# Attention stage of a hybrid decoder step: order of turns, scores and minima in each quarter, and a new split of the PSUM banks

## The chip, the cores and the metric

The kernel runs on one core of one Trainium2 chip. The metric is the device time of one launch in microseconds (us), lower is better. Engines are called PE (TensorE; PEld is its weight load), DVE (VectorE), ACT (ScalarE), POOL (GpSimd) and SP (SyncE).

## The reference, cut to what matters

One layer of a Hymba-style decoder over a prompt of 1024 tokens and a sample batch of 8 x 4 tokens. The change touches only the prompt's attention:

```
qs = q * (HEAD_DIM ** -0.5)
# per head and block of 128 queries:
o_cmp = softmax(qs k_cmp + bias, masked) v_cmp          # 16 compressed blocks
o_sel = softmax(qs k_sel + bias, masked) v_sel          # selected blocks; 16 blocks, so all are selected
o_win = softmax(qs k_win + bias, masked) v_win          # 512 back plus the own block
out   = g0 * o_cmp + g1 * o_sel + g2 * o_win            # g = sigmoid gates; 16 heads of 64
mix   = out * silu(z_a)
```

All is in fp32; the score products use a high and a low part of the keys.

## The kernel before, in words

Before the stage come the projections (up to 890 us of the span) and the compressed blocks; after it the sample's attention and the output projection (from 1443 us). The prompt's attention lies between.

**Units.** The stage has NU = 32 units. Unit u works on 4 heads (pass u // 8 of four) and the 128 queries of block i = TILE_ORDER[u % 8], in the order 0, 2, 4, 6, 7, 5, 3, 1. Each unit has two halves, numbered w: w = 2u is the selected branch with i + 1 tiles of 128 keys, w = 2u + 1 is the window branch with min(i + 1, 5) tiles and one tile for the compressed blocks (`tiles_of`, `keys_of`). So a pass has 74 tiles. Each half is cut into four quarters h = 0 to 3, one for each head's scores, and the half's tiles are dealt out over the quarters (`slots`).

**What is done for a half w.** `scores(w, h)`, on PE, multiplies one head's queries with up to 1024 keys into a score buffer. `maxima(w, h)`, on DVE, adds the bias to the last 256 columns and takes the minimum (scores are negated); `exps(w, h)`, on ACT, takes the exponential into the SBUF tile pr and the sum. When all four heads are done, `factors(w)`, on DVE, makes gate over sum, and `scale` multiplies pr by it: heads 0 and 1 on POOL, 2 and 3 on ACT. Then `turn_p(w, t)`, on PE, transposes the four heads' 128 columns of tile t into a PSUM bank ("turned"), `copy_p(w, t)` copies this bank to the SBUF tile ptt (even tiles on ACT, odd ones on DVE), and `values(w, t)`, on PE, multiplies it with the values into the unit's result bank. `gate_o(u)`, on DVE, multiplies the finished result with silu(z_a) into mixs, which SP stores.

**Order.** Every engine runs a fixed program, in order; semaphores link them. The loop runs over w and h. While half w is turned, half w + 2 is scored, and half w + 1 is scaled. In each quarter PE does `scores(w + 2, h)`, then the quarter's `turn_p`, then a batch of `values` for tiles that are held back (all but one once five are held, and what is left of the unit before in quarter 2 of a selected half). DVE does `maxima(w + 2, h)`, then its copies, then in quarter 0 or 1 `factors(w + 1)` (quarter 1 where w is even), and `gate_o` in quarter 3 of a selected half. ACT does its copies, then `exps(w + 2, h)`, then in quarters 1 and 2 its share of `scale(w + 1)`. POOL follows with `scale(w + 1)`. The turning of half w waits at its first tile for both shares of its scaling (n_act, n_pool).

**PSUM.** There are 8 banks of 512 fp32 columns. Before: score buffers are two pairs of banks, 0-1 and 2-3, taken in turn, so that a score waits for the exponential of the score two before it (e_done); turned tiles take banks 4 and 5 in turn, so that a turning waits for the copy of the tile two before it; results take banks 6 and 7 in turn.

Of the kernel before, what the change touches and what calls it, by code (L numbers as in the profile page):

```python
# [11 lines left out]
ALU = mybir.AluOpType  # L12
ACT = mybir.ActivationFunctionType
# [5 lines left out]
P = 128  # L19
D = 1024  # L20
S = 1024
# [28 lines left out]
CB = 2 * P + NPB + 1  # L50


NPT5 = 6
TILE_ORDER = (0, 2, 4, 6, 7, 5, 3, 1)
NWE = 6

# [1 line left out]
def build(nc: "bass.Bass", x_prompt, x_sample, cache_k_cmp, cache_v_cmp, cache_k_slc, cache_v_slc, cache_k_win,  # L58
# [10 lines left out]
    def sb(name, shape, dt=F32, cx=None):  # L69
        return (cx or ctx).enter_context(nc.sbuf_tensor(name, shape, dt))  # L70
# [15 lines left out]
    with ctx:  # L86
        PS = ctx.enter_context(nc.psum_tensor("PS", [P, 8, 512], F32))
# [10 lines left out]
        ident = sb("ident", [P, P])  # L98
# [83 lines left out]
        c4 = ExitStack()  # L182
        ksh, ksl, kwh, kwl = (sb(n, [P, NG, S], F32R, c4) for n in ("ksh", "ksl", "kwh", "kwl"))
        pr2 = sb("pr2", [P, 4, S], cx=c4)
        sb("spare", [P, 4, S], cx=c4)
        edge = sb("edge", [P, P], cx=c4)
        edger = sb("edger", [P, P], F32R, c4)
        identr = sb("identr", [P, P], F32R, c4)
# [9 lines left out]
        pt = [sb(f"ptt{i}", [P, 4, P], cx=c4) for i in range(NPT5)]  # L198
        zau = [sb(f"zau{i}", [P, 2, P], cx=c4) for i in range(2)]
        mixs = [sb(f"mixs{i}", [P, 2, P], cx=c4) for i in range(2)]  # L200
# [116 lines left out]
        NI = 2 * NU  # L317
# [14 lines left out]
        def keys_of(w):  # L332

            k = (tiles_of(w) - w % 2) * P
            return k, {5: [384, 256], 6: [512, 256], 7: [384, 512], 8: [512, 512]}.get(k // P, [k])

        def score_cols(b0, w):

            k, parts = keys_of(w)
            lo = 512 - parts[0] if len(parts) > 1 else 0  # L340
            return PS[:, b0:b0 + 2, :].rearrange("p a b -> p (a b)")[:, lo:lo + k]

# [4 lines left out]
        def slots(w):  # L347

            n = tiles_of(w)
            cuts = [(n * q + 2) // 4 for q in range(5)]  # L350
            return [range(cuts[q], cuts[q + 1]) for q in range(4)]

        def turned(c):

            return (pt_dve if c % 2 else pt_act), c // 2 + 1
# [353 lines left out]
        def _(pe):  # L709
# [149 lines left out]
            def scores(w, h):  # L859
                u, n, g = w // 2, 4 * w + h, h // 2  # L860
                i = unit(u)[1]
                if h == 0:
                    pe.wait_ge(q_ld[u % 4], 16 * (u // 4 + 1))
                if n >= 2:
                    pe.wait_ge(e_done, n - 1)
                b0 = 2 * (n % 2)
                q = qb[u % 4][:, h, :]
                kh, kl = (ksh, ksl) if w % 2 == 0 else (kwh, kwl)
                k, parts = keys_of(w)
                a = (i + 1) * P - k  # L870
# [12 lines left out]
                ins.then_inc(s_mm, 1)  # L883

            def turn_p(w, t):
                tc = tile0[w] + t
                if t == 0:
                    pe.wait_ge(n_act, w + 1)
                    pe.wait_ge(n_pool, w + 1)
                if w % 2 and t == tiles_of(w) - 1:  # L890
                    pe.wait_ge(c_pool, w // 2 + 1)
                if tc >= 2:
                    pe.wait_ge(*turned(tc - 2))
                for h in range(4):
                    cmp_ = w % 2 and t == tiles_of(w) - 1
                    src = prc[w % 3][:, h, :] if cmp_ else pr[w % 3][:, h, t * P:(t + 1) * P]
                    ins = pe.transpose(PS[:, 4 + tc % 2, h * P:(h + 1) * P], src, ident[:, :])  # L897
                ins.then_inc(t_mm, 1)

            def values(w, t):  # L900
                tc, u = tile0[w] + t, w // 2
                i = unit(u)[1]
                pe.wait_ge(*turned(tc))
                first, last = w % 2 == 0 and t == 0, w % 2 == 1 and t == tiles_of(w) - 1
                if first and u >= 2:
                    pe.wait_ge(r_ev, u - 1)
                for g in range(NG):
                    if last:
                        v = vcp[:, g, :]
                    elif w % 2:  # L910
                        v = kvt[:, max(0, i - 4) + t, C_VW + HD * g:C_VW + HD * g + HD]
                    else:
                        v = kvt[:, t, C_VS + HD * g:C_VS + HD * g + HD]
                    ins = pe.matmul(PS[64 * g:64 * g + 64, 6 + u % 2, 0:2 * P], v, pt[tc % NPT5][:, 2 * g:2 * g + 2, :].rearrange("p j c -> p (j c)"), start=first, stop=last)  # L914
                ins.then_inc(pv_mm, 1)

            pe.wait_ge(nr_rdy, 2)
# [5 lines left out]
            held = []  # L923
            for w in range(NI):
                for h, part in enumerate(slots(w)):
                    if w + 2 < NI:
                        scores(w + 2, h)
                    for t in part:
                        turn_p(w, t)
                        held.append((w, t))  # L930
                    old = [x for x in held if x[0] < w - w % 2] if h == 2 else []
                    go = max(len(old), len(held) - 1 if len(held) >= 5 else 0)
                    for x in held[:go]:
                        values(*x)
                    held = held[go:]
# [133 lines left out]
        def _(act):  # L1069
# [118 lines left out]
            def exps(w, h):  # L1188
                n, u = 4 * w + h, w // 2
                i = unit(u)[1]  # L1190
                act.wait_ge(m_rdy, n + 1)
                if h == 0 and w >= 3:
                    act.wait_ge(t_mm, tile0[w - 2])
                k, parts = keys_of(w)
                b0, r = 2 * (n % 2), w % 3
                act.activation(pr[r][:, h, 0:k], score_cols(b0, w), ACT.Exp, scale=-1.0, bias=nm[:, r, h:h + 1], accum_out=rsum[:, r, h:h + 1]).then_inc(e_done, 1)  # L1196

            def exp_first(u):
# [12 lines left out]
            def copy_p(w, t):  # L1211
                tc = tile0[w] + t
                act.wait_ge(t_mm, tc + 1)
                if tc >= NPT5:
                    act.wait_ge(pv_mm, tc - NPT5 + 1)
                act.activation(pt[tc % NPT5][:, :, :], PS[:, 4 + tc % 2, :].rearrange("p (h c) -> p h c", h=4), ACT.Copy).then_inc(pt_act, 1)  # L1216

            keys_high(0)
            for w in range(2):
# [109 lines left out]
        def _(dve):  # L1329
# [169 lines left out]
            def maxima(w, h):  # L1499
# [5 lines left out]
                    dve.wait_ge(n_pool, w - 2)  # L1505
                    dve.wait_ge(c_pool, (w - 2) // 2)
                k, parts = keys_of(w)
                b0, r = 2 * (n % 2), w % 3
                both = w % 2 and h == 3
                if both:  # L1510
                    if u:
# [39 lines left out]
            def copy_p(w, t):  # L1551
                tc = tile0[w] + t
                dve.wait_ge(t_mm, tc + 1)
                if tc >= NPT5:
                    dve.wait_ge(pv_mm, tc - NPT5 + 1)
                dve.tensor_copy(pt[tc % NPT5][:, :, :], PS[:, 4 + tc % 2, :].rearrange("p (h c) -> p h c", h=4)).then_inc(pt_dve, 1)  # L1556

            def gate_o(u):
                dve.wait_ge(pv_mm, tile0[2 * u + 2])
                dve.wait_ge(za_ld[u % 2], 16 * (u // 2 + 1))  # L1560
                if u >= 2:
                    dve.wait_ge(mix_st[u % 2], 16 * (u // 2))
                dve.tensor_tensor(mixs[u % 2][:, :, :], PS[:, 6 + u % 2, 0:2 * P].rearrange("p (j c) -> p j c", j=2), zau[u % 2][:, :, :], ALU.mult).then_inc(r_ev, 1)

            for w in range(2):
                for h in range(4):
# [4 lines left out]
                    dve.wait_ge(nr_rdy, 4)  # L1571
            for w in range(NI):
                for h, part in enumerate(slots(w)):
                    if w + 2 < NI:
                        maxima(w + 2, h)
                    for t in part:
                        if (tile0[w] + t) % 2:
                            copy_p(w, t)
                    if w + 1 < NI:
                        if h == (w + 1) % 2:  # L1580
                            factors(w + 1)
                    if h == 3 and w % 2 == 0 and w:
                        gate_o(w // 2 - 1)
            gate_o(NU - 1)
            dve.wait_ge(pv_mm, tile0[NI])
            dve.wait_ge(mix_st[0], 16 * NU // 2)
# [203 lines left out]
```

## Time and profile before

| | us |
|---|---|
| runs (3), median | 1819.63 (1819.53 to 1823.33) |
| profiled execution, its time | 1816.56 |
| profiled execution, its span | 1814.8 |
| PE busy over the span | 1595.9 (88%) |
| DVE, ACT, POOL busy | 792.5, 633.9, 317.1 |
| attention stage | 892 to 1443 us of the span |

The profiled execution has 1.8 us around its span and lies 3.1 us below the median of the runs. A busy time is the sum of an engine's instructions; idle time of an engine matters only where the other engines' work does not cover it.

### The profile page before, as it was taken

The numbers are of one execution on the slowest core, as the hardware profiler recorded it, in microseconds if no ns is written. First come the engines' busy times: TensorE is split into PE (matmuls) and PEld (weight loads), VectorE is DVE, ScalarE is ACT, GpSimd is POOL, SyncE is SP. The second block draws the span as 40 slices with busy tenths as digits, with TensorE's granted clock in tenths as the row PEclk, the third lists the DMA queues.
The fourth block names the chain that finished last, engine by engine and source line by source line (L and its number), as shares of the span: only waits on it lengthen the run. The fifth ranks groups of instructions, "written<-read, shape, count | busy, mean of one in ns | idle before, by whom it ended". The sixth has DMA issues, their size and how long they took to land.

```text
span 1814.8 us, 24776 instructions
## 1 busy us (share of the span) xinstructions
PE 1595.9 (88%) x9752; PEld 1339.1 (74%) x9752; DVE 792.5 (44%) x1859; ACT 633.9 (35%) x1261; POOL 317.1 (17%) x377
## 2 busy tenths in 40 slices
PE   5799899999999999699589889889889757689995
PEld 1397899999999999687467667667577535468883
DVE  0343212212222122355576676677577457543221
ACT  0122111111111111145567667667567423331110
POOL 2000300000000000210044344344344311000000
PEclk9899899999999999899789999999999968899998
DMA  7417832232222322483101110110110265453220
GB/s 252 143 49 88 264 94 59 71 86 71 77 71 70 94 71 59 154 275 112 55 24 42 36 36 24 36 36 24 36 36 25 71 232 172 136 174 97 94 66 18
DMA packets 166776, 164.58 MB, mean 91 GB/s; under 512 B 48178, under 2 KB 143026, under 8 KB 162363
## 3 DMA queue, kind: packets, MB, share of 16 engines
q1 hardware_dynamic: 151956, 93.46, 18.4%
q0 software_dynamic: 14704, 69.53, 12.3%
q8 instruction: 78, 1.28, 0.3%
q14 instruction: 38, 0.31, 0.1%
HBM read 131.28 MB, written 35.83 MB: 92 GB/s over the span
## 4 chain that ended last, share of the span: by engine, by line
PE 75%; DVE 10%; DMA 6%; ACT 4%; issue 4%; SPq 0%; POOL 0%; DVEq 0%; ACTq 0%
PE PS L784 30%; PE PS L1062 10%; PE PS L914 8%; PE PS L897 5%; PE PS L874 4%; PE PS L821 3%; PE PS L875 2%; DMA adaw<-in_ada_w 2%; PE PS L721 2%; PE PS L758 2%; DMA wr<-in_w_in 2%; DVE nm L1518 2%; PE PS L760 2%; ACT pr L1196 2%; PE PS L759 2%
## 5 line engine op out<-in xcount | busy, mean ns | idle before, releaser
L784 PE MATMUL PS<-hhi,wh 128*128 128x352 f32 x1152 | 251.3, 326 | 8.4 <-DVE wl L1401 6.7
L784 PE MATMUL PS<-hhi,wl 128*128 128x352 f32 x1152 | 249.2, 324 | 0.0
L784 PE MATMUL PS<-hlo,wh 128*128 128x352 f32 x1152 | 249.0, 324 | 0.0
L672 POOL TENSOR_SCALAR pr<-pr,rg 128x640 f32<-128x640 f32 (+7 forms) x128 | 203.9, 1605 | 226.5 <-DVE rg L1549 144.6
L1196 ACT ACTIVATE pr<-PS,nm 128x640 f32<-128x640 f32 (+7 forms) x256 | 179.0, 699 | 108.7 <-DVE nm L1519 99.1
L784 PEld LDWEIGHTS PS<-hhi,wh 128*128 128x128 f32 x1152 | 196.9, 190 | 9.6 <-issue 9.0
L784 PEld LDWEIGHTS PS<-hhi,wl 128*128 128x128 f32 x1152 | 198.7, 189 | 0.0
L784 PEld LDWEIGHTS PS<-hlo,wh 128*128 128x128 f32 x1152 | 196.5, 188 | 0.0
L897 PE MATMUL PS<-ident,pr 128*128 128x128 f32 x1056 | 154.4, 280 | 17.1 <-DVE ptt L1556 8.6
L897 PEld LDWEIGHTS PS<-ident,pr 128*128 128x128 f32 x1056 | 122.8, 143 | 36.8 <-DVE ptt L1556 16.2
L1518 DVE TENSOR_REDUCE nm<-PS 128x1 f32<-128x384 f32 (+5 forms) x192 | 106.2, 553 | 81.5 <-PE PS L875 80.0
L914 PE MATMUL PS<-ptt,kvt 128*64 128x256 f32 x1056 | 134.9, 394 | 0.0
L1401 DVE TENSOR_TENSOR wl<-wr,wh 128x1024 fp32r<-128x1024 f32 x48 | 58.6, 1220 | 172.0 <-ACT wh L1116 171.4
L1216 ACT ACTIVATE ptt<-PS 128x512 f32<-128x512 f32 x148 | 87.5, 591 | 71.1 <-PE PS L897 70.8
L874 PE MATMUL PS<-kwh,qb 128*128 128x384 f32 (+3 forms) x192 | 78.1, 407 | 36.1 <-ACT pr L1196 24.3
L1116 ACT ACTIVATE wh<-wr 128x1024 fp32r<-128x1024 f32 x48 | 50.6, 1055 | 168.8 <-PE PS L784 151.4
L1556 DVE COPY ptt<-PS 128x512 f32<-128x512 f32 x148 | 101.6, 687 | 8.8 <-PE PS L897 8.5
L914 PEld LDWEIGHTS PS<-ptt,kvt 128*64 128x64 f32 x1056 | 72.0, 140 | 42.0 <-issue 13.4
L874 PE MATMUL PS<-ksh,qb 128*128 128x384 f32 (+3 forms) x192 | 80.0, 418 | 20.2 <-ACT pr L1196 10.8
L1519 DVE CUSTOM_DVE_ANT_0 PS<-PS,near,nm 128x256 f32<-128x256 f32 x192 | 94.6, 493 | 6.8
L1207 ACT ACTIVATE pr<-pr,rg 128x640 f32<-128x640 f32 (+7 forms) x128 | 93.5, 731 | 7.1 <-DVE rg L1549 6.6
L1062 PE MATMUL PS<-woh,mh 128*128 128x512 f32 (+1 forms) x288 | 90.1, 394 | 6.0 <-DVE ml L1699 5.9
(280 smaller groups left out, 2440.0 us busy)
## 6 DMA issues: line engine op xcount, KB each, us to landing
wr<-in_w_in SPq DMA_DIRECT2D x32, 512.0 KB, 4.2
adaw<-in_ada_w SPq DMA_DIRECT2D x6, 2048.0 KB, 9.1
wr<-in_w_in SPq DMA_DIRECT2D x32, 256.0 KB, 3.5
qb<-q_stacked SPq DMA_DIRECT2D x32, 256.0 KB, 3.1
mr<-mixed SPq DMA_DIRECT2D x16, 512.0 KB, 3.8
mixed<-ych POOLq DMA_DIRECT2D x8, 528.0 KB, 3.3
z_attn_silu<-zab POOLq DMA_DIRECT2D x8, 528.0 KB, 3.0
xb<-in_x_prompt POOLq DMA_DIRECT2D x8, 512.0 KB, 3.7
```

The costliest lines, as they stand in the source:

```text
L672: ins = po.tensor_scalar(pr[r][:, h, 0:k], pr[r][:, h, 0:k], rg[:, r, h:h + 1], None, ALU.mult)
L784: ins = pe.matmul(PS[:, bank + c, 0:CH], a[kind % 2][:, k, :], b[:, k, c * CH:(c + 1) * CH], start=(k == 0 and b is hhi and a is wh), stop ...
L874: pe.matmul(PS[:, b0 + c, x:x + m], q, kh[:, g, a:a + m], start=True, stop=False)
L897: ins = pe.transpose(PS[:, 4 + tc % 2, h * P:(h + 1) * P], src, ident[:, :])
L914: ins = pe.matmul(PS[64 * g:64 * g + 64, 6 + u % 2, 0:2 * P], v, pt[tc % NPT5][:, 2 * g:2 * g + 2, :].rearrange("p j c -> p (j c)"), start ...
L1062: ins = pe.matmul(PS[0:n, b0 + c, :], a[:, k, 0:n], b[k][:, 512 * c:512 * c + 512], start=(k == 0 and a is mh and b is woh), stop=(k == 15 ...
L1196: act.activation(pr[r][:, h, 0:k], score_cols(b0, w), ACT.Exp, scale=-1.0, bias=nm[:, r, h:h + 1], accum_out=rsum[:, r, h:h + 1]).then_inc ...
L1207: ins = act.activation(pr[r][:, h, 0:k], pr[r][:, h, 0:k], ACT.Copy, scale=rg[:, r, h:h + 1])
L1216: act.activation(pt[tc % NPT5][:, :, :], PS[:, 4 + tc % 2, :].rearrange("p (h c) -> p h c", h=4), ACT.Copy).then_inc(pt_act, 1)
L1518: link(dve.tensor_reduce(low, cols[:, 0:far], AX.X, ALU.min))
L1519: dve.tensor_tensor_reduce(cols[:, far:k], cols[:, far:k], near[:, head_of(u, h), 2 * P - (k - far):2 * P], 1.0, low if far else 3.0e38, A ...
L1556: dve.tensor_copy(pt[tc % NPT5][:, :, :], PS[:, 4 + tc % 2, :].rearrange("p (h c) -> p h c", h=4)).then_inc(pt_dve, 1)
```

## The change

Four things. First, in each quarter PE turns first and scores second, and DVE copies first and takes minima second; ACT's and POOL's programs keep their order. Second, the four score banks become a ring: a score of at most 512 keys takes one bank (except the fourth head of a window half, which also holds the compressed scores), others take two aligned ones; `score_prior` names the last score that held the bank, and PE waits for its exponential. Third, turned tiles take three banks (4, 5, 7) and results one bank (6): the first `values` of a unit waits for `gate_o` of the unit before. Fourth, for that, PE flushes the held tiles of the unit before in quarter 0 (or 1) of a selected half, and DVE does `gate_o` at the start of quarter 1. The SBUF ring of copied tiles grows from 6 to 8.

```diff
-NPT5 = 6
+NPT5 = 8
...
+        score_bank, score_prior, at, held_by = [], [], 0, {}
+        for n in range(4 * NI):
+            two = keys_of(n // 4)[0] > 512 or n % 8 == 7
+            at = (at + at % 2) % 4 if two else at
+            banks = (at, at + 1) if two else (at,)
+            score_bank.append(at)
+            score_prior.append(max(held_by.get(b, -1) for b in banks))
+            held_by.update((b, n) for b in banks)
+            at = (at + len(banks)) % 4
+
         def score_cols(b0, w):
 
             k, parts = keys_of(w)
+            if len(parts) == 1:
+                return PS[:, b0, 0:k]
...
+        def turn_bank(c):
+
+            return (4, 5, 7)[c % 3]
...
-                if n >= 2:
-                    pe.wait_ge(e_done, n - 1)
-                b0 = 2 * (n % 2)
+                if score_prior[n] >= 0:
+                    pe.wait_ge(e_done, score_prior[n] + 1)
+                b0 = score_bank[n]
...
-                if tc >= 2:
-                    pe.wait_ge(*turned(tc - 2))
+                if tc >= 3:
+                    pe.wait_ge(*turned(tc - 3))
...
-                if first and u >= 2:
-                    pe.wait_ge(r_ev, u - 1)
+                if first and u:
+                    pe.wait_ge(r_ev, u)
...
             for w in range(NI):
                 for h, part in enumerate(slots(w)):
-                    if w + 2 < NI:
-                        scores(w + 2, h)
                     for t in part:
                         turn_p(w, t)
                         held.append((w, t))
-                    old = [x for x in held if x[0] < w - w % 2] if h == 2 else []
-                    go = max(len(old), len(held) - 1 if len(held) >= 5 else 0)
+                    if w + 2 < NI:
+                        scores(w + 2, h)
+                    old = [x for x in held if x[0] < w - w % 2]
+                    go = len(old) if w % 2 == 0 and h < 2 else len(held) - 1 if len(held) >= 5 else 0
                     for x in held[:go]:
                         values(*x)
                     held = held[go:]
...
             for w in range(NI):
                 for h, part in enumerate(slots(w)):
-                    if w + 2 < NI:
-                        maxima(w + 2, h)
+                    if h == 1 and w % 2 == 0 and w:
+                        gate_o(w // 2 - 1)
                     for t in part:
                         if (tile0[w] + t) % 2:
                             copy_p(w, t)
+                    if w + 2 < NI:
+                        maxima(w + 2, h)
                     if w + 1 < NI:
                         if h == (w + 1) % 2:
                             factors(w + 1)
-                    if h == 3 and w % 2 == 0 and w:
-                        gate_o(w // 2 - 1)
```

In the rows below, ksh and ksl are the selected branch's keys, kwh and kwl the window's, qb the queries; L874/L875 (now L890/L891) are scores, L897 (now L913) turnings, L914 (now L930) values, L1518/L1519 (L1534/L1535, "ISA") minima, L1556 (L1572) copies on DVE, L1542 to L1549 (L1558 to L1565) factors, L1563 (L1579) `gate_o`.

PE, from the first turning of the selected half of block i = 3 (w = 12 of the first pass; the same stands in each pass) to its second. Before:

```order
L874 MATMUL PS<-ksh,qb 128x256 [waits e_done,q_ld3]
L875 MATMUL PS<-ksl,qb 128x256
L897 MATMUL PS<-ident,pr 128x128 [waits pt_act,n_pool,n_act]
L897 MATMUL PS<-ident,pr 128x128 x3
L874 MATMUL PS<-ksh,qb 128x256 [waits e_done]
L875 MATMUL PS<-ksl,qb 128x256
L897 MATMUL PS<-ident,pr 128x128 [waits pt_dve]
L897 MATMUL PS<-ident,pr 128x128 x3
```

The same place now:

```order
L913 MATMUL PS<-ident,pr 128x128 [waits pt_dve,n_pool,n_act]
L913 MATMUL PS<-ident,pr 128x128 x3
L890 MATMUL PS<-ksh,qb 128x256 [waits e_done,q_ld3]
L891 MATMUL PS<-ksl,qb 128x256
L930 MATMUL PS<-ptt,kvt 64x256 [waits pt_act]
...
L930 MATMUL PS<-ptt,vcp 64x256 [waits pt_dve]
L930 MATMUL PS<-ptt,vcp 64x256
L913 MATMUL PS<-ident,pr 128x128 [waits pt_act]
L913 MATMUL PS<-ident,pr 128x128 x3
L890 MATMUL PS<-ksh,qb 128x256 [waits e_done]
L891 MATMUL PS<-ksl,qb 128x256
```

Four held tiles' values (eight instructions) now stand between the scores of head 0 and the turning and scores of head 1; before they stood ahead of this piece.

DVE at the same place, from the minimum of head 0 to the factors of the next half. Before:

```order
L1519 ISA PS,nm<-PS,near 128x256 [waits n_pool,c_pool,n_act,s_mm]
L1519 ISA nm 128x1
L1519 ISA PS,nm<-PS,near 128x256 [waits s_mm]
L1519 ISA nm 128x1
L1556 COPY ptt<-PS 128x512 [waits pv_mm,t_mm]
L1541 TENSOR_REDUCE rsum<-prc 128x4 [waits ec_done,e_done]
L1542 RECIPROCAL rrec<-rsum 128x8 [waits dch]
L1548 TENSOR_TENSOR rg<-rrec,sg 128x4 [waits dch]
L1549 TENSOR_TENSOR rg<-rrec,sg 128x4 [waits dch]
```

and now:

```order
L1535 ISA PS,nm<-PS,near 128x256 [waits n_pool,c_pool,n_act,s_mm]
L1535 ISA nm 128x1
L1579 TENSOR_TENSOR mixs<-PS,zau 128x256 [waits mix_st1,za_ld1,pv_mm]
L1572 COPY ptt<-PS 128x512 [waits pv_mm,t_mm]
L1535 ISA PS,nm<-PS,near 128x256 [waits s_mm]
L1535 ISA nm 128x1
L1557 TENSOR_REDUCE rsum<-prc 128x4 [waits ec_done,e_done]
L1558 RECIPROCAL rrec<-rsum 128x8 [waits dch]
L1564 TENSOR_TENSOR rg<-rrec,sg 128x4 [waits dch]
L1565 TENSOR_TENSOR rg<-rrec,sg 128x4 [waits dch]
```

Before, head 1's minimum came first, then the copy, then the factors; now `gate_o` and the copy stand ahead of head 1's minimum, and `gate_o` waits for the batch of values (pv_mm).

PE at the turn to the selected half of block i = 2 (w = 2). Before:

```order
L874 MATMUL PS<-kwh,qb 128x384 [waits e_done]
L875 MATMUL PS<-kwl,qb 128x384
L882 MATMUL PS<-kcp,qb 128x32 x4
L874 MATMUL PS<-ksh,qb 128x384 [waits e_done,q_ld2]
L875 MATMUL PS<-ksl,qb 128x384
L874 MATMUL PS<-ksh,qb 128x256
L875 MATMUL PS<-ksl,qb 128x256
L897 MATMUL PS<-ident,pr 128x128 [waits pt_dve,n_pool,n_act]
L897 MATMUL PS<-ident,pr 128x128 x3
```

and now:

```order
L890 MATMUL PS<-kwh,qb 128x384 [waits e_done]
L891 MATMUL PS<-kwl,qb 128x384
L898 MATMUL PS<-kcp,qb 128x32 x4
L913 MATMUL PS<-ident,pr 128x128 [waits pt_act,n_pool,n_act]
L913 MATMUL PS<-ident,pr 128x128 x3
L890 MATMUL PS<-ksh,qb 128x384 [waits e_done,q_ld2]
L891 MATMUL PS<-ksl,qb 128x384
L890 MATMUL PS<-ksh,qb 128x256
L891 MATMUL PS<-ksl,qb 128x256
```

The first score of the coming half now stands behind a turning that waits for both shares of the scaling.

## Rows read from the trace of the kernel before

**Rows 1.** The page, its first part: busy us, share, instructions.

```profile
PE 1595.9 (88%) x9752; PEld 1339.1 (74%) x9752; DVE 792.5 (44%) x1859; ACT 633.9 (35%) x1261; POOL 317.1 (17%) x377
```

**Rows 2.** Windows: stretch us, busy of PE, PEld, DVE, ACT, POOL, clock, DMA.

```profile
911.00:1440.00 529.00, 475.02 (x3286) 356.90 (x3288) 361.84 (x1151) 349.25 (x801) 219.86 (x218) 0.96 0.12 32
1072.70:1152.30 79.60, 74.84 (x544) 56.06 (x542) 57.79 (x166) 55.75 (x111) 35.84 (x29) 1.00 0.10 27
1152.30:1158.40 6.10, 4.26 (x30) 3.06 (x29) 4.78 (x19) 4.35 (x13) 3.15 (x3) 1.00 0.00 1
1158.40:1166.80 8.40, 8.10 (x64) 5.72 (x64) 3.19 (x11) 4.41 (x13) 2.27 (x5) 1.00 0.24 65
1166.80:1203.90 37.10, 29.95 (x200) 23.05 (x200) 25.76 (x99) 23.91 (x68) 14.12 (x20) 0.95 0.15 44
```

**Rows 3.** Waits of PE, 911 to 1440 us: total us, times, longest.

```profile
PE PS L874 <- ACT pr L1196: 33.2, 47, 1.2
PE PS L897 <- DVE ptt L1556: 8.9, 21, 0.9
PE PS L897 <- ACT pr L1207: 4.0, 4, 1.0
PE PS L897 <- POOL pr L672: 2.7, 2, 2.4
PE PS L897 <- ACT ptt L1216: 1.8, 8, 0.3
```

**Rows 4.** Timeline, second pass, selected half of block 3: start us, us, instruction, [idle].

```profile
1152.31 0.46 PEld L897 LDWEIGHTS PS<-ident,pr 128*128 128x128 f32 x4
...
1152.74 0.19 PEld L874 LDWEIGHTS PS<-ksh,qb 128*128 128x128 f32 x1
...
1153.29 0.43 DVE L1519 CUSTOM_DVE_ANT_0 PS<-PS,near 128x256 f32<-128x256 f32 x1 [0.19 <-PE PS L875]
...
1153.73 0.69 DVE L1556 COPY ptt<-PS 128x512 f32<-128x512 f32 x1
...
1154.98 0.16 DVE L1549 TENSOR_TENSOR rg<-rrec,sg 128x4 f32<-128x4 f32 x1
1155.02 0.20 PEld L914 LDWEIGHTS PS<-ptt,vcp 128*64 128x64 f32 x4 [0.17 <-issue]
...
1155.25 3.11 POOL L672 TENSOR_SCALAR pr<-pr,rg 128x512 f32<-128x512 f32 x2 [3.66 <-DVE rg L1549]
...
1155.60 0.19 PEld L874 LDWEIGHTS PS<-ksh,qb 128*128 128x128 f32 x1 [0.39 <-issue]
...
1156.98 0.36 PE L874 MATMUL PS<-kwh,qb 128*128 128x256 f32 x1 [0.44 <-ACT pr L1196]
...
1158.42 0.42 PEld L897 LDWEIGHTS PS<-ident,pr 128*128 128x128 f32 x4 [1.17 <-ACT pr L1207]
```

**Rows 5.** Timeline of PE: a batch of four tiles' values and the score behind it.

```profile
1190.34 1.08 PE L914 MATMUL PS<-ptt,kvt 128*64 128x256 f32 x8
...
1192.22 0.44 PE L874 MATMUL PS<-ksh,qb 128*128 128x384 f32 x1
```

**Rows 6.** Timeline at the end of block 2's selected half, second to third pass.

```profile
1194.30 0.79 ACT L1196 ACTIVATE pr<-PS,nm 128x640 f32<-128x640 f32 x1 [1.35 <-DVE nm L1519]
...
1195.08 0.60 ACT L1207 ACTIVATE pr<-pr,rg 128x384 f32<-128x384 f32 x1
...
1195.32 0.41 PE L874 MATMUL PS<-kwh,qb 128*128 128x384 f32 x1 [1.22 <-ACT pr L1196]
...
1196.00 0.46 PEld L897 LDWEIGHTS PS<-ident,pr 128*128 128x128 f32 x4
```

**Rows 7.** Timeline of PE: a score of 128 keys that waits for its pair of banks.

```profile
1170.64 0.30 PE L874 MATMUL PS<-kwh,qb 128*128 128x128 f32 x1 [0.84 <-ACT pr L1196]
```

**Rows 8.** Windows as in rows 2: the same half of a unit in three passes.

```profile
1035.30:1046.10 10.80, 10.05 (x46) 7.36 (x44) 3.88 (x17) 2.79 (x12) 1.48 (x4) 0.54 0.17 48
1171.50:1178.30 6.80, 5.64 (x45) 4.24 (x43) 3.66 (x17) 2.88 (x11) 1.48 (x4) 1.00 0.26 73
1302.60:1312.70 10.10, 8.89 (x46) 6.25 (x43) 3.82 (x18) 2.94 (x12) 1.48 (x4) 0.66 0.18 51
```

More of the change, by code:

```diff
@@ L184, in build @@
         pr2 = sb("pr2", [P, 4, S], cx=c4)
-        sb("spare", [P, 4, S], cx=c4)
+        sb("spare", [P, 3 * S], cx=c4)
         edge = sb("edge", [P, P], cx=c4)
@@ L896, in turn_p @@
                     src = prc[w % 3][:, h, :] if cmp_ else pr[w % 3][:, h, t * P:(t + 1) * P]
-                    ins = pe.transpose(PS[:, 4 + tc % 2, h * P:(h + 1) * P], src, ident[:, :])
+                    ins = pe.transpose(PS[:, turn_bank(tc), h * P:(h + 1) * P], src, ident[:, :])
                 ins.then_inc(t_mm, 1)
@@ L913, in values @@
                         v = kvt[:, t, C_VS + HD * g:C_VS + HD * g + HD]
-                    ins = pe.matmul(PS[64 * g:64 * g + 64, 6 + u % 2, 0:2 * P], v, pt[tc % NPT5][:, 2 * g:2 * g + 2, :].rearrange("p j c -> p (j c)"), start=first, stop=last)
+                    ins = pe.matmul(PS[64 * g:64 * g + 64, 6, 0:2 * P], v, pt[tc % NPT5][:, 2 * g:2 * g + 2, :].rearrange("p j c -> p (j c)"), start=first, stop=last)
                 ins.then_inc(pv_mm, 1)
@@ L1194, in exps @@
                 k, parts = keys_of(w)
-                b0, r = 2 * (n % 2), w % 3
+                b0, r = score_bank[n], w % 3
                 act.activation(pr[r][:, h, 0:k], score_cols(b0, w), ACT.Exp, scale=-1.0, bias=nm[:, r, h:h + 1], accum_out=rsum[:, r, h:h + 1]).then_inc(e_done, 1)
@@ L1215, in copy_p @@
                     act.wait_ge(pv_mm, tc - NPT5 + 1)
-                act.activation(pt[tc % NPT5][:, :, :], PS[:, 4 + tc % 2, :].rearrange("p (h c) -> p h c", h=4), ACT.Copy).then_inc(pt_act, 1)
+                act.activation(pt[tc % NPT5][:, :, :], PS[:, turn_bank(tc), :].rearrange("p (h c) -> p h c", h=4), ACT.Copy).then_inc(pt_act, 1)
             keys_high(0)
@@ L1507, in maxima @@
                 k, parts = keys_of(w)
-                b0, r = 2 * (n % 2), w % 3
+                b0, r = score_bank[n], w % 3
                 both = w % 2 and h == 3
@@ L1555, in copy_p @@
                     dve.wait_ge(pv_mm, tc - NPT5 + 1)
-                dve.tensor_copy(pt[tc % NPT5][:, :, :], PS[:, 4 + tc % 2, :].rearrange("p (h c) -> p h c", h=4)).then_inc(pt_dve, 1)
+                dve.tensor_copy(pt[tc % NPT5][:, :, :], PS[:, turn_bank(tc), :].rearrange("p (h c) -> p h c", h=4)).then_inc(pt_dve, 1)
             def gate_o(u):
@@ L1562, in gate_o @@
                     dve.wait_ge(mix_st[u % 2], 16 * (u // 2))
-                dve.tensor_tensor(mixs[u % 2][:, :, :], PS[:, 6 + u % 2, 0:2 * P].rearrange("p (j c) -> p j c", j=2), zau[u % 2][:, :, :], ALU.mult).then_inc(r_ev, 1)
+                dve.tensor_tensor(mixs[u % 2][:, :, :], PS[:, 6, 0:2 * P].rearrange("p (j c) -> p j c", j=2), zau[u % 2][:, :, :], ALU.mult).then_inc(r_ev, 1)
             for w in range(2):
```

## The prediction

> **What bounds the kernel now.** I read the page first, then windows over the attention stage, then PE's waits there, then single stretches in order of time. The page says that PE is busy 88% of the span and DVE, ACT and POOL far less [rows 1]. The change touches only the prompt's attention. There PE is busy 475.0 of 529.0 us, DVE 361.8, ACT 349.3, POOL 219.9 [rows 2]: PE sets the pace, and its 54 us of idle time are all that a new order can win. PE's waits name the causes: 33.2 us before scores, for the exponential that frees a pair of score banks; 8.9 + 1.8 = 10.7 us before turnings, for a copy that frees a turned bank; 4.0 + 2.7 = 6.7 us before turnings for the scaling of pr [rows 3].
>
> A pass takes about 131 us, and its stretches have different limits. I cut the second pass into three. **Stretch A**, blocks 4, 6, 7, 5, takes 79.6 us with PE busy 74.8: PE is the limit. **Stretch B**, block 3, takes 6.1 + 8.4 us; in the first part PE is busy 4.26 of 6.1. **Stretch C**, block 1 and then blocks 0 and 2 of the next pass, takes 37.1 us with PE busy 29.95 [rows 2]: here, and in the first part of B, something else is the limit.
>
> What it is in B can be read off the timeline. The first turning of block 3's selected half starts at 1152.31. Head 1's score starts at 1152.74 and its minimum at 1153.29; behind it on DVE stand a copy (0.69) and the factors, the last at 1154.98; POOL scales two heads from 1155.25 for 3.11; the window half's first turning starts at 1158.42 after PE sat idle 0.99 to 1.17 us [rows 4]. The profile names ACT there, but ACT had long been done: POOL ended at 1158.36. So this half is a chain, **turn, score, minimum, factors, scaling, turn**, of 6.1 us, and not a matter of PSUM banks.
>
> **The change part by part.** Added work is small: the instructions of turning, score, minimum, copy and exponential are the same in number, and only the batches of values are cut otherwise, into 87 in place of 79 (counted by the loop's rule), two or so more per pass.
>
> *Copies first, three turned banks.* In A a turning waited for a copy that stood behind a minimum on DVE. With copies first and a third bank I let this go wholly: 10.7 us over the stage, 2.7 per pass [rows 3]. If a copy is late again, it is late by less than a minimum. Against it stand the two more batches. A batch of four tiles takes 1192.22 - 1190.34 = 1.88 us [rows 5], one of a single tile 1155.60 - 1155.02 = 0.58 [rows 4], each after a gap of 0.17; so 0.43 per tile and 0.15 + 0.17 = 0.32 per batch, 0.6 per pass. **A: -2.1 per pass.** The trace has values only between turnings and scores; the new order puts them between scores and turnings. The weight load's gap behind a batch is 0.39 [rows 4], of which PE streams the last matmuls; between nothing more and 0.39 us more for each of 87 batches (34 us, were PE the limit everywhere) I take nothing, since the streaming must end in either order, and keep 10 us for the upper end.
>
> *One result bank, flush in quarter 0.* This is the dear part. With one bank the values left from the unit before must be out before `gate_o`, and they are flushed in quarter 0, in front of head 1's turning and score, which feed the chain of B. `gate_o` (some 0.4 us on DVE) is hidden there by PE's next turning. In B four tiles are flushed. The chain becomes: turning 0.43; head 0's score 0.3; batch 0.17 + 1.88 = 2.05; turning 0.43; then DVE's copy, which now stands before head 1's minimum, 0.28 (the signal, estimated from the same timeline) + 0.69 = 0.97, longer than the score beside it (0.55 from its start to the minimum); minimum and factors 1155.25 - 1153.29 - 0.69 = 1.27; POOL and signal 1158.42 - 1155.25 = 3.17 [rows 4]. Sum 8.6 us in place of 6.1. The half behind it has two batches before and now, is PE's (8.1 of 8.4 [rows 2]) and may lose its 0.3 to 0.4 of idle time. **B: +2.1 per pass.** In C the selected half of block 1 has the same chain, with one tile flushed in it: 0.17 + 0.58 = 0.75. In A the chains are longer too, but PE's own work there (74.8 of 79.6) covers them; if it did not, block 4's selected half would lose most, up to 1 us per pass.
>
> *Turn first, score second.* The first turning of a half waits for the last head's scaling on ACT, and that stands behind the third head's exponential. Before, the next score needed only this exponential: it ended at 1195.09, the score went at 1195.32, and the scaling ran beside it, 1195.08 to 1195.68. Now the turning goes first: it starts after 1195.68 + 0.1, takes 0.46, and the score follows at 1196.24 [rows 6], 0.92 us later; with it the next minimum and exponential, which pace these small halves. Where a batch of values lies between, it is covered; in C four borders between halves per pass have none (block 0's two halves and block 2's). 4 x 0.92 = 3.7.
>
> *Single score banks.* They help only where 512 keys or fewer are scored, and there they remove waits like the 0.84 us of [rows 7] and the 0.44 us before the window score in [rows 4]. Most of the 33.2 us come back as the wait for the scaling above, because that chain is the longer one. I count these two, 1.3 per pass; the lower end would be all idle time of C, 7 us. **C: 0.8 + 3.7 - 1.3 = +3.2 per pass.**
>
> **The sum.** -2.1 + 2.1 + 3.2 = +3.2 us per pass, four passes: +12.8. The profiled execution's 1816.56 becomes 1829.4; it lies 3.1 us below the median of the runs, so the median would be about **1832**.
>
> **A rule against this forecast.** The trace says that C's idle time sits in a chain over three engines. The Trainium skill, Perfetto Trace Analysis, "Identifying Performance Opportunities", reads it otherwise: the same gap again and again on the engine that should be saturated can mean that buffers ran out. By that rule the change, which adds score and turned buffers, would win. The trace agrees for the 10.7 us of copy waits and for the names of the 33.2 us [rows 3], not for the first part of B [rows 4].
>
> **The rivals.** *Faster: the buffers were the limit.* The copy waits (10.7 us) go, and of the 33.2 us before scores the part at single banks, say a third, 11 us; the flush in quarter 0 is caught up later, because DVE and ACT are idle a third of the time. About 1816.6 - 22 + 3 = 1798 at best, half of it likelier: 1808. For it: [rows 3], and a pipeline two halves deep. Against: the chain in [rows 4] has no slack to catch up in. It wins if stretch B stays under 15 us. Chance 0.25.
>
> *No change.* A's gain and C's loss are both half right, 1819 to 1823. Half of the units, and 50 of 74 tiles in a pass, have scores of over 512 keys, where the ring is the old pair of buffers, so this part of the change does nothing there. Chance 0.1.
>
> *Slower still: the clock.* The same half of a unit took 6.8 us at a granted clock of 1.00, but 10.8 at 0.54 and 10.1 at 0.66 [rows 8]; the clock fell from its 2.4 to its 1.2 GHz level in C, behind the halves in which PE was busy about two thirds of the time. If the idle time that I expect in B and C (5 us more per pass) draws such a fall in each pass, it costs 3.3 to 4.0 us more in each, 13 to 16 in all: 1847. The Trainium skill, TensorE: Matmul & The Clock Gate, "A second HAM failure mode: psum-queue depth-cycling", tells of such a loss where PE idles briefly between groups while it cycles through PSUM banks. The trace agrees that the falls come where PE waits for banks. Chance 0.13.
>
> **How the numbers follow.** My forecast has 0.52, at 1832, its own range 1822 to 1842. The range that should hold the time 8 times in 10 reaches from the likely half of the faster case to the clock case: 1807 to 1848. A measurement of this kernel tells about 0.2% (3.6 us) from no change. Faster by more than that: the first rival, 0.25. Within: 0.1. Slower: 0.52 + 0.13 = 0.65.
>
> **What would show each step.** In the new profile: PE's waits on copies at L913 near 0; waits on ACT and POOL scaling at L913 above 20 us in all, where they were 6.7; block 3's two halves 16 to 17 us in place of 14.5, with POOL's scaling starting some 5.4 us after the first turning; blocks 4, 6, 7, 5 at 77 to 78 us; waits on exponentials well under 33 us. The forecast is wrong if the waits at L913 for scaling stay small, if block 3 keeps its 14.5 us, or if the stage (551 us) is shorter than before.

## The result: 1.9% slower

The changed kernel takes 1854.8 us (median of 4 runs, 1852.86 to 1857.25), the one before 1820.08 (4 runs): ratio 1.0186, 95% interval 1.0169 to 1.0202, so 34.7 us slower. The profiled execution took 1852.86 us, with a span of 1851.1. I forecast slower, at 1832 with 1807 to 1848: the sign was right, the size not, and the time lies above the range.

The page's first part, after; it answers to [rows 1]:

```profile
PE 1592.0 (86%) x9752; PEld 1339.1 (72%) x9752; DVE 795.9 (43%) x1859; ACT 636.6 (34%) x1261; POOL 317.1 (17%) x377
```

All engines are busy for about as long as before. The loss is PE's idle time, and a lower granted clock. A granted clock of 1.00 in a row is the 2.4 GHz level throughout; below it a part of the stretch ran at 1.2 GHz. The windows, after, cut as in [rows 2] (the whole stage, stretch A, the two halves of block 3, stretch C; columns: stretch us, busy of PE, PEld, DVE, ACT, POOL, clock, DMA share, GB/s):

```profile
911.00:1476.00 565.00, 475.62 (x3298) 360.57 (x3300) 367.43 (x1161) 354.51 (x810) 221.31 (x221) 0.93 0.11 30
1084.80:1164.40 79.60, 73.10 (x537) 54.92 (x537) 57.77 (x162) 55.25 (x109) 35.60 (x28) 1.00 0.10 27
1164.40:1172.80 8.40, 4.96 (x40) 3.80 (x40) 4.32 (x19) 5.21 (x15) 3.39 (x4) 1.00 0.22 63
1172.80:1182.30 9.50, 9.37 (x64) 6.64 (x64) 3.79 (x15) 4.62 (x13) 2.29 (x5) 0.82 0.01 2
1182.30:1227.80 45.50, 33.17 (x194) 25.82 (x192) 26.62 (x100) 24.07 (x68) 14.13 (x20) 0.81 0.13 35
```

Stretch A takes 79.6 us as before, where I had 77.5. Block 3's selected half takes 8.4 (before 6.1), its window half 9.5 (before 8.4), now at a clock of 0.82. Stretch C takes 45.5 in place of 37.1, at 0.81 in place of 0.95. From the first turning to the last the stage takes 559.2 us, where it took 527.6: 31.6 us of the loss. It also starts 4 us later in this execution, in code that the change does not touch.

PE's waits in the stage, after (total us, times, longest), against [rows 3]:

```profile
PE PS L913 <- ACT pr L1223: 67.9, 40, 3.5
PE PS L890 <- ACT pr L1212: 14.8, 14, 1.8
PE PS L930 <- ACT ptt L1232: 1.8, 4, 0.5
PE PS L913 <- POOL pr L688: 1.6, 1, 1.6
PE PS L913 <- ACT ptt L1232: 1.1, 4, 0.3
```

The waits moved as forecast: for copies 10.7 to 1.1 us, for exponentials 33.2 to 14.8, for the scaling 6.7 to 69.5. The last is more than the first two gave.

The chain of block 3, after, in order of time (start us, us, instruction, idle before it):

```profile
1164.39 0.42 PEld L913 LDWEIGHTS PS<-ident,pr 128*128 128x128 f32 x4 [1.36 <-ACT pr L1223]
...
1164.79 0.19 PEld L890 LDWEIGHTS PS<-ksh,qb 128*128 128x128 f32 x1
...
1165.22 1.51 PE L930 MATMUL PS<-ptt,kvt 128*64 128x256 f32 x12
...
1167.10 0.42 PEld L913 LDWEIGHTS PS<-ident,pr 128*128 128x128 f32 x4 [0.38 <-issue]
...
1167.80 0.69 DVE L1572 COPY ptt<-PS 128x512 f32<-128x512 f32 x1 [0.16 <-PE PS L913]
...
1168.40 0.42 DVE L1535 CUSTOM_DVE_ANT_0 PS<-PS,near 128x256 f32<-128x256 f32 x1
...
1169.65 3.10 POOL L688 TENSOR_SCALAR pr<-pr,rg 128x512 f32<-128x512 f32 x2 [4.49 <-DVE rg L1565]
...
1172.83 0.47 PEld L913 LDWEIGHTS PS<-ident,pr 128*128 128x128 f32 x4 [3.68 <-ACT pr L1223]
```

It is the forecast chain: from turning to POOL's start 5.26 us, where [rows 4] show 2.94, and PE stands still for 3.5 us at its end. In the window half behind it the clock falls, in three of the four passes; in the first pass it stays up, and block 3 takes 16.3 us there in place of 17.9.

### The profile page after: what moved, and what is told of

Same layout as the page of the kernel before. It is cut to its first block, busy times and chain, and to the rows that moved or that the text cites. A ratio compares the mean times of both kernels' runs of the same rounds, so it can differ in the third digit from the quotient of the medians.

```text
span 1851.1 us, 24774 instructions
## 1 busy us (share of the span) xinstructions
PE 1592.0 (86%) x9752; PEld 1339.1 (72%) x9752; DVE 795.9 (43%) x1859; ACT 636.6 (34%) x1261; POOL 317.1 (17%) x377
## 4 chain that ended last, share of the span: by engine, by line
PE 71%; DVE 11%; ACT 6%; DMA 6%; issue 5%; SPq 0%; POOL 0%; DVEq 0%; ACTq 0%
PE PS L800 29%; PE PS L1078 9%; PE PS L930 6%; PE PS L913 6%; PE PS L837 3%; PE PS L890 2%; DVE nm L1534 2%; PE PS L891 2%; DMA adaw<-in_ada_w 2%; ACT pr L1212 2%; ACT pr L1223 2%; PE PS L737 2%; PE PS L774 2%; DMA wr<-in_w_in 2%; PE PS L776 1%
## 5 line engine op out<-in xcount | busy, mean ns | idle before, releaser
L913 PE MATMUL PS<-ident,pr 128*128 128x128 f32 x1056 | 159.6, 287 | 71.1 <-ACT pr L1223 67.9
L913 PEld LDWEIGHTS PS<-ident,pr 128*128 128x128 f32 x1056 | 119.4, 145 | 114.9 <-ACT pr L1223 83.5
L930 PE MATMUL PS<-ptt,kvt 128*64 128x256 f32 x1056 | 143.1, 414 | 1.8 <-ACT ptt L1232 1.8
L1572 DVE COPY ptt<-PS 128x512 f32<-128x512 f32 x148 | 101.9, 689 | 76.3 <-PE PS L913 76.1
L1534 DVE TENSOR_REDUCE nm<-PS 128x1 f32<-128x384 f32 (+5 forms) x192 | 105.9, 552 | 57.6 <-PE PS L891 57.2
L930 PEld LDWEIGHTS PS<-ptt,kvt 128*64 128x64 f32 x1056 | 73.4, 146 | 50.6 <-issue 16.7
L1535 DVE CUSTOM_DVE_ANT_0 PS<-PS,near,nm 128x256 f32<-128x256 f32 x192 | 94.6, 493 | 6.8
L890 PE MATMUL PS<-ksh,qb 128*128 128x384 f32 (+3 forms) x192 | 78.2, 409 | 17.9 <-DVE ksl L1503 9.6
L890 PE MATMUL PS<-kwh,qb 128*128 128x384 f32 (+3 forms) x192 | 77.2, 403 | 17.6 <-DVE kwl L1503 9.1
```

The source lines that it names most:

```text
L913: ins = pe.transpose(PS[:, turn_bank(tc), h * P:(h + 1) * P], src, ident[:, :])
L930: ins = pe.matmul(PS[64 * g:64 * g + 64, 6, 0:2 * P], v, pt[tc % NPT5][:, 2 * g:2 * g + 2, :].rearrange("p j c -> p (j c)"), start=first, ...
L1534: link(dve.tensor_reduce(low, cols[:, 0:far], AX.X, ALU.min))
L1535: dve.tensor_tensor_reduce(cols[:, far:k], cols[:, far:k], near[:, head_of(u, h), 2 * P - (k - far):2 * P], 1.0, low if far else 3.0e38, A ...
L1572: dve.tensor_copy(pt[tc % NPT5][:, :, :], PS[:, turn_bank(tc), :].rearrange("p (h c) -> p h c", h=4)).then_inc(pt_dve, 1)
```

## Experiments

Twelve kernels ran, each timed beside the kernel before, on three chips. The ratios compare each with the kernel before on its own chip; the plain times of two kernels can differ by a microsecond or two more from chip to chip (the kernel before: 1820.1 to 1822.5). In the table, A, B and C are the stretches of the second pass (for C the range over the first three passes, in the profiled executions), read at the first turning of the halves; "half clock" is the time in the stage at the 1.2 GHz level. All columns from A on come from one profiled execution each.

| kernel | us | ratio (95%) | A | B | C | half clock |
|---|---|---|---|---|---|---|
| before | 1820.1 | 1 | 79.6 | 14.5 | 37.1 to 42.1 | 44 |
| changed | 1854.8 | 1.0186 (1.0169 to 1.0202) | 79.6 | 17.9 | 41.9 to 45.8 | 72 |
| o_only | 1876.0 | 1.0304 (1.0286 to 1.0323) | 89.5 | 17.2 | 40.0 to 42.9 | 95 |
| o_ring | 1877.8 | 1.0314 (1.0297 to 1.0332) | 89.5 | 17.2 | 39.9 to 40.2 | 103 |
| banks_only | 1816.9 | 0.9976 (0.9961 to 0.9990) | 74.8 | 19.4 | 38.8 to 41.1 | 64 |
| ring_only | 1825.3 | 1.0025 (1.0008 to 1.0043) | 79.6 | 16.1 | 40.3 to 41.5 | 57 |
| after_fill | 1832.9 | 1.0056 (1.0036 to 1.0076) | 79.8 | 16.4 | 39.7 to 40.9 | 12 |
| score_first_q0 | 1830.6 | 1.0061 (1.0039 to 1.0084) | 77.3 | 17.7 | 39.3 to 42.4 | 70 |
| flush_q1 | 1831.1 | 1.0044 (1.0025 to 1.0063) | 78.1 | 14.3 | 43.9 to 44.2 | 75 |
| both_undone | 1801.7 | 0.9885 (0.9845 to 0.9926) | 76.7 | 14.1 | 37.7 to 39.5 | 42 |
| banks_flush_q1 | 1797.7 | 0.9872 (0.9849 to 0.9896) | 74.0 | 14.7 | 37.7 to 40.2 | 32 |
| turned_flush_q1 | 1803.0 | 0.9886 (0.9844 to 0.9928) | 74.4 | 15.0 | 40.3 to 40.5 | 44 |
| q1_fill | 1787.8 | 0.9811 (0.9771 to 0.9851) | 74.1 | 14.7 | 37.1 to 37.2 | 14 |
| before_fill | 1825.4 | 1.0025 (1.0015 to 1.0035) | 79.6 | 14.5 | 40.5 | 9 |

### The four parts alone

**o_only**: the kernel before with the new order and nothing else, on PE and in the same way on DVE.

```diff
-                    if w + 2 < NI:
-                        scores(w + 2, h)
                     for t in part:
                         turn_p(w, t)
                         held.append((w, t))
+                    if w + 2 < NI:
+                        scores(w + 2, h)
```

> Only the order is changed: turn and copy first, score and minimum second; banks, flush and the result gate stay as before. Order theory (a half's first turning, which waits for the scaling, now stands in front of the next score): slower than before by 10 to 25 us, and block 3's two halves keep 14.5 us. Flush theory (the batch of values in front of head 1's score makes the loss): within 5 us of before. Either way more than 20 us of waits for the scaling at the turnings if the order theory holds.

It is the dearest of all: 3.0% slower, and the loss sits in the big blocks, 9.9 us a pass in stretch A. PE's waits in its stage:

```profile
PE PS L897 <- ACT pr L1207: 34.4, 23, 2.1
PE PS L897 <- ACT ptt L1216: 31.0, 20, 2.4
PE PS L897 <- POOL pr L672: 13.9, 6, 2.5
```

To the waits for the scaling (48.3 us) come 31.0 us for copies on ACT. ACT's program is unchanged: a quarter's copy stands behind the last quarter's exponential, and with only two turned banks the early turning runs into it. The order theory had the mechanism, the waits for the scaling, but not the size: the order costs 55 us without the third turned bank, over twice the upper end of what I expected. Part of that is the clock, which falls here in the big blocks as well (95 us at half clock in the stage, 44 before). Block 3's halves take 14.3 to 17.2 us, 17.2 only where the clock is down in them.

**banks_only**: the changed kernel with the old order, so all banks, the early flush and the early gate.

> The changed kernel with PE's and DVE's old order (score and minimum first); ring of score banks, three turned banks, one result bank, early flush and early gate stay. Flush theory: block 3 still takes about 17 us a pass, 8 to 14 us slower than before in all. Order theory: close to before, within 5 us.

Faster than before by 0.24% (0.10 to 0.39%): within the 5 us of the order theory, and not the 8 to 14 us slower of the flush theory. In stretch A most of the idle time is gone; block 3 pays for the flush, and for the clock:

```profile
1074.00:1148.70 74.70, 73.23 (x536) 55.49 (x534) 56.77 (x159) 56.09 (x109) 35.65 (x28) 1.00 0.11 29
1148.70:1168.20 19.50, 15.82 (x105) 11.22 (x105) 8.82 (x35) 9.65 (x28) 5.67 (x8) 0.82 0.10 29
```

So the banks give 4.8 us a pass in A, and the flush in quarter 0 takes 4.9 in B (2.0 in the pass where the clock stayed up, 16.5 us). In A the ring of score banks does nothing (**ring_only**, 79.6), and one result bank can only add a wait, so the gain there is the third turned bank's, together with the eight slots for copied tiles; no run parts these two, but in the kernel before no wait of a copy for the values that free its slot shows in the trace. Together with **o_only** this shows that the two big parts of the change work against each other, and that the order is the loss: 55 us alone, and 38 us on top of the banks (1816.9 to 1854.8).

**ring_only**: the kernel before with `score_bank` and `score_prior` alone.

> The kernel before with the ring of score banks alone. If score banks were a limit at 512 keys or fewer: 4 to 10 us faster than before, PE's waits on exponentials down from 33 to about 20 us. If the chain of minimum and exponential is the limit: within 3 us.

PE's waits for exponentials fell to 21.9 us as forecast, but those for the scaling rose from 6.7 to 25.4, and the time by 0.25% (0.08 to 0.43%). PE scores earlier and then stands at the next wait. The slowdown itself may be the clock's alone: there are 13 us more at half clock, and in the pass where the clock stays up in block 3, it takes 14.5 us as before.

**o_ring**: new order and ring, two turned and two result banks, old flush.

> New order and ring of score banks, with two turned and two result banks, the old flush and the old gate. Order theory: like the order alone or up to 5 us better. Flush theory: within 5 us of before; block 3 at about 14.5 us in both theories. The difference to the changed kernel is the price of the one result bank with its early flush: 8 to 15 us.

No better than the order alone. The change's step from here is the third turned bank with its price, one result bank and the early flush: it brings 23 us (1877.8 to 1854.8), where I expected it to cost 8 to 15.

### The two costs, and the clock

**after_fill**: the changed kernel, with idle transposes ahead of the waits for the scaling.

```diff
                 tc = tile0[w] + t
+                if tc >= 3:
+                    pe.wait_ge(*turned(tc - 3))
                 if t == 0:
+                    for _ in range({13: 28, 15: 20, 1: 26, 2: 8, 3: 12}.get(w % 16, 0) if w > 1 else 0):
+                        pe.transpose(PS[:, turn_bank(tc), 0:P], ident[:, :], ident[:, :])
                     pe.wait_ge(n_act, w + 1)
                     pe.wait_ge(n_pool, w + 1)
```

> The changed kernel; in five of sixteen halves PE transposes the identity 8 to 28 times into the free turned bank before it waits for the scaling, so that it is busy in the longest of these waits. The output is the same. Clock theory (idle stretches of 2 to 4 us make the clock fall, and a good part of the 35 us is work at 1.2 GHz): half-clock time in the stage falls from 72 us to under 40, time falls by 10 to 18 us. If the clock is a by-product only: within 4 us of the changed kernel.

Its windows (the stage, A, B, C):

```profile
911.00:1456.00 545.00, 488.76 (x3655) 382.11 (x3656) 367.19 (x1162) 354.78 (x812) 221.75 (x221) 0.98 0.11 31
1080.10:1159.90 79.80, 73.06 (x536) 54.98 (x536) 57.81 (x162) 55.32 (x109) 35.65 (x28) 1.00 0.10 27
1159.90:1176.30 16.40, 15.76 (x132) 12.60 (x132) 8.13 (x34) 9.86 (x28) 5.70 (x8) 1.00 0.13 33
1176.30:1217.20 40.90, 35.00 (x260) 29.68 (x258) 26.29 (x102) 23.92 (x68) 14.17 (x20) 0.96 0.14 40
```

With more work for PE and the same semaphores to wait for, the time falls by 22 us (1.3% of the kernel before; 20.2 us in the profiled stage), and the half-clock time from 72 to 12 us. With the clock up the changed kernel's B is 16.4 us and its C 39.7 (40.9 in the pass that still has 3.4 us at half clock). These 22 us are not the clock's share of the 34.7, since the kernel before also spends 44 us of its stage at half clock. A fair comparison takes the kernel before where its clock was up as well: B 14.5 us, and C 37.1 in its best pass. Against these **after_fill** loses 0.7 us in A, 7.7 in B and 9.1 in C (over all passes), and 3.1 in blocks 0 and 2 of the first pass and block 1 of the last: some 20 us are the new waits' own. The stage lost 31.6 us, so some 11 us of it are the clock's, an estimate, because its base for C is one pass of the kernel before.

**score_first_q0**: the changed kernel with score and minimum first again in quarter 0 only.

```diff
+                    if h == 0 and w + 2 < NI:
+                        scores(w + 2, h)
                     for t in part:
                         turn_p(w, t)
                         held.append((w, t))
-                    if w + 2 < NI:
+                    if h and w + 2 < NI:
                         scores(w + 2, h)
```

> The changed kernel, but in quarter 0 of each half score and minimum come first again, as before the change; quarters 1 to 3 keep the new order. Border theory (only the score in front of a half's first, waiting turning matters): 15 to 30 us faster than the changed kernel. If the order costs in every quarter: under 10 us faster.

24 us faster than the changed kernel, as the border theory said. The score in front of the first, waiting turning is worth 2.3 us a pass in A (77.3); in C the three passes change by +0.4, -6.2 and -3.4 us, and B becomes longer in two passes (18.9), both with the clock falling at other places. The half-clock time as a whole stays (70 us).

**flush_q1**: the changed kernel, flush one quarter later, gate one quarter later.

```diff
-                    go = len(old) if w % 2 == 0 and h < 2 else len(held) - 1 if len(held) >= 5 else 0
+                    go = len(old) * h if w % 2 == 0 and h < 2 else len(held) - 1 if len(held) >= 5 else 0
...
-                    if h == 1 and w % 2 == 0 and w:
+                    if h == 2 and w % 2 == 0 and w:
```

> The changed kernel with the left-over values flushed in quarter 1, behind head 1's score, and the result gate in quarter 2. Flush theory: block 3's selected half falls from 8.4 to about 6.4 us, 8 to 12 us faster in all. Else within 4 us of the changed kernel.

Block 3's selected half, in its windows:

```profile
1161.90:1168.30 6.40, 4.94 (x40) 3.77 (x40) 4.44 (x19) 5.38 (x15) 3.42 (x4) 1.00 0.17 47
```

6.4 us, as expected, but 24 us faster in all, twice what I expected: B falls from 17.9 to 14.3, since without the 3.5 us wait its window half keeps its clock, and A by 1.5. C does not gain in the mean of its three passes (44.1 against 44.4), and the stage still has 75 us at half clock.

**both_undone** has both edits on the changed kernel.

> The changed kernel with both costs mended: score and minimum first in quarter 0, flush in quarter 1, gate in quarter 2; in quarters 1 to 3 turn and copy stay first. If these two and the clock are the whole loss: about 1800 us, like banks_flush_q1. If turning and copying first costs in the big blocks as well: stretch A near 76 to 77 us in place of 74.0, and 1808 to 1815 us.

1801.7 us: 53 us under the changed kernel. A is 76.7, so turning and copying first in quarters 1 to 3 costs another 2.7 us a pass against **banks_flush_q1** (below), in the big blocks: the second forecast's mechanism. The border theory thus has the larger part of the order's price, but not all of it. The profiled stage is 10.1 us longer than that of **banks_flush_q1**; by the ratios (0.9885 and 0.9872) the two can't be told apart, and the time came out nearer to the first forecast.

### Which parts are worth keeping

**banks_flush_q1**: all banks of the change, the old order, flush in quarter 1, gate in quarter 2.

> All the banks of the changed kernel with the old order, flush in quarter 1 and gate in quarter 2. If the third turned bank is worth 4.8 us a pass in blocks 4, 6, 7, 5 and the early flush is what gives it back in block 3: 74.8 and about 14.5 us there, about 1800 us in all, faster than before by 15 to 22 us. If the late gate holds up the values: within 5 us of before.

1.3% faster than before; A and B in its windows:

```profile
1068.40:1142.40 74.00, 73.07 (x536) 56.01 (x534) 56.60 (x162) 55.78 (x109) 35.65 (x28) 1.00 0.11 30
1142.40:1157.10 14.70, 12.87 (x104) 9.50 (x104) 8.81 (x35) 9.66 (x28) 5.70 (x8) 1.00 0.13 38
```

PE is busy 73.1 of 74.0 us in A, and block 3 pays next to nothing (14.7 against 14.5).

**turned_flush_q1** is the same with the pairs of score banks of before (`two = True`).

> As banks_flush_q1, but the score buffers are the two pairs of before: what is left of the change are the third turned bank, the single result bank and the flush in quarter 1. If the ring of score banks is worth nothing: within 4 us of banks_flush_q1 (1797.7). If it helps at small blocks: 5 to 10 us slower than that, the loss in blocks 1, 0 and 2.

5.3 us slower than **banks_flush_q1**, but the intervals overlap (0.9844 to 0.9928 against 0.9849 to 0.9896), so by the times alone the ring's worth is open. In the profiles the stage is 7.9 us longer, some 5 of it in blocks 1, 0 and 2, but with 12 us more at half clock, so that the ring and the clock are not parted here either. The third turned bank and the late flush bring the gain; what the ring is worth stays open, between nothing and these 8 us.

**q1_fill** is **banks_flush_q1** with 10, 14 and 20 idle transposes ahead of the three turnings of a pass that still waited 1.3 to 2.5 us (w % 16 = 13, 15, 1).

> As banks_flush_q1, with 10, 14 and 20 idle transposes of the identity ahead of the three turnings of a pass that still wait 1.3 to 2.5 us for the scaling. Clock theory: half-clock time in the stage (31.8 us) falls below 15, and the time by 4 to 8 us, to about 1792. Else within 3 us.

```profile
911.00:1412.00 501.00, 472.18 (x3453) 368.98 (x3452) 363.78 (x1164) 356.02 (x812) 221.78 (x221) 0.98 0.12 34
```

1787.8 us, 1.9% under the kernel before and the best of all; half-clock time 14 us, C 37.1 to 37.2 in every pass. The time is 9.9 us lower than that of **banks_flush_q1**, on another chip; the profiled stage is 6.4 us shorter, within the 4 to 8 us of the clock theory.

**before_fill**: the kernel before with seven idle transposes ahead of each score of four halves.

> The kernel before with seven idle transposes (0.7 us) ahead of each score in four halves of a pass (window half of block 1, both of block 0, selected half of block 2), where PE waits for exponentials. If the clock also costs the kernel before: half-clock time in its stage falls from 43.6 us to under 25 and the time by 4 to 12 us, and the distance of the filled changed kernel (1832.9) to it is the loss at equal clock, 15 to 25 us. If the idle transposes delay the scores more than the clock gives: within 4 us of before, or slower.

The clock stayed up (half-clock time 9 us), and yet the kernel became 0.25% slower: C is 40.5 in every pass, above the 37.1 of its best pass before. Here the transposes stand ahead of scores, which feed the chain that paces this stretch, and may hold them up; that this is what gives the clock's gain back fits the times, but no run shows it by itself. So this run doesn't give the clean price at equal clock that I wanted from it; the 7.4 us between it and **after_fill** mix both.

## Why the prediction was wrong

**What bounds the stage**: right. PE paces A in the kernel before, a chain of turning, score, minimum, factors and POOL's scaling paces block 3, and its length came out as worked out: 8.6 us forecast, 8.44 measured (1164.39 to 1172.83). Block 1's half, forecast 0.75 us longer, became 0.84 longer.

**"A: -2.1 per pass"**: wrong, 0; this is the first step that failed, worth 8.4 us over four passes. The removed copy waits were right (10.7 us to 1.1). What failed is the sentence that PE's own work covers the longer chains there. In the window of A, before, PE waited for copies and exponentials, and no wait of PE names the scaling:

```profile
PE PS L897 <- DVE ptt L1556: 2.1, 5, 0.9
PE PS L874 <- ACT pr L1196: 1.6, 2, 1.0
PE PS L897 <- ACT ptt L1216: 0.5, 2, 0.3
```

After, it waits for the scaling at five turnings:

```profile
PE PS L913 <- ACT pr L1223: 5.6, 5, 1.4
PE PS L890 <- ACT pr L1212: 0.9, 1, 0.9
```

I counted the turning behind the scaling only at borders in C; in A it costs 2.3 us (**score_first_q0**), and the rest of the new order 2.7 (**both_undone** against **banks_flush_q1**). What the third bank is worth I undersized: 4.8 us a pass in the old order, where I had 2.7 less 0.6 for the batches. Gain and price cancel.

**"One result bank, flush in quarter 0: +2.1"**: right with the clock up, 1.9 (16.4 us in **after_fill**; 1.8 in the changed kernel's first pass), but measured 3.4 in the other three.

**"Turn first, score second: +3.2 in C"**: 2.6 to 3.8 with the clock up or nearly so (39.7 to 40.9 in **after_fill** against 37.1), so about right; measured -0.2, +8.4 and +4.7 in the three passes against the same passes before. These differences carry the clock on both sides: the kernel before had 17, 3 and 14 us at half clock in its three passes, the changed one 10, 17 and 17.

**The sum.** B and C, forecast at +8.4 and +12.8 us over four passes, came out at some 8 and 12 with the clock up. With A at nothing in place of -8.4 the sum would have been 21 us, and that is the some 20 us that **after_fill** shows beside the kernel before at its own high clock. That **after_fill** itself, 10.4 us above the runs of before beside it, looks like the 12.8 us forecast is luck: A's missing gain and the falls of the kernel before offset each other there.

**The clock**: the second step that failed. I had it as a rival with a chance of 0.13 and 13 to 16 us on top, and put it at nothing in the likeliest sum, though the sum itself put waits of over 3 us where PE was already idle a third of the time and [rows 8] showed what a fall costs. The half-clock time in the stage rose from 44 to 72 us, not evenly: in the first pass block 3 kept its clock and C had less of it than before; the other passes have more. The price is some 11 us net (all falls of the changed kernel together 20 to 22 us by **after_fill**, less what those of the kernel before cost). So the rival had the size about right, and its chance was too low.

Either step alone would have left the time inside my range (about 1840 or 1843 us); both together give about 1851. The other 3 or 4 us lie outside the stage, where nothing was changed. The sign was right, and so was the mechanism in B and C; in A it was not.

**The rule on buffers**: it is half right here. More score buffers alone, where waits named them, made the kernel 0.25% slower (**ring_only**), and beside the other banks they brought at most 8 us (**turned_flush_q1**), each time with more time at half clock where the kernel was slower, so what they are worth by themselves is open; the one more turned bank brought 19 us in A. [rows 3] showed 33.2 us for the first and 10.7 for the second. So the size of a named wait did not tell its worth; which stretch it was in told more: where PE was the limit, the bank was worth its wait and more. That agrees with the Trainium skill, Perfetto Trace Analysis, "Optimization Strategy", which wants gaps looked for within one regime.

## What to carry to other kernels

In a program with fixed order on each engine, don't put an instruction that waits long in front of one that feeds the next round: turning first cost 55 us alone and 38 with the new banks, and 24 of the changed kernel's 35 came back when one score per half stood in front of it again. Work that hides nothing (here a batch of values) belongs behind the instruction that starts the longest chain; one quarter later was worth 24 us too. Where new waits are forecast on TensorE, put the fall of its clock into the likeliest sum, and test it with idle work in the waits, but only in waits that something else ends. And compare a kernel whose clock is kept up only with one that has its clock up too.

## What the runs showed of the hardware

Idle transposes in waits kept the clock up and made two kernels faster: **after_fill** by 22 us (20.2 in the profiled stage, for 60 us less at half clock) and **q1_fill** by 10 us (6.4 in the stage, for 18 us less). Keeping the clock up was not enough by itself: **before_fill** had only 9 us at half clock and was 0.25% slower than the kernel before.

The two mends bring 24 and 24 us alone and 53 together. Neither lowers the half-clock time by itself (70 and 75 us against 72), but both together do (42 us), which may be the surplus; the rest of the difference is within what plain times on several chips can tell.

And the clock fell in the kernel before, too: in the window 1035 to 1060 us it had two falls, and the longest single wait of PE there was 1.1 us:

```profile
PE PS L874 <- ACT pr L1196: 3.4, 4, 1.1
```

The Trainium skill, TensorE: Matmul & The Clock Gate, "A second HAM failure mode: psum-queue depth-cycling", describes that pattern of short idles, and the trace agrees.
